# Rotating retention's keys and queries beside the input projection: halves swapped by DMA, products on GpSimd

## The reference, cut to what matters

```
q = _rotary(rq, pos)                       # (x1, x2) -> (x1 cos - x2 sin, x1 sin + x2 cos)
k = _rotary(rk, pos) * HEAD_DIM ** -0.5    # x1, x2: first and second half of each head's 64
for each chunk of 128 tokens, per head:
    att = (q @ k.T) * dmat
    o = att @ v + (q @ s) * q_dec
    s = s * c_dec + (k * k_dec).T @ v
```

## Time and profile before

| | us |
|---|---|
| median of 3 runs | 1070.62 |
| lowest, highest | 1069.22, 1072.57 |
| the profiled execution's own time | 1070.89 |
| its span, first to last instruction | 1069.1 |
| PE busy in the span | 974.4 (91%) |
| DVE busy | 628.9 (59%) |
| ACT busy | 344.7 (32%) |
| POOL busy | 109.6 (10%) |
| mean granted PE clock, as a share of full speed | 0.956 |
| data moved, mean rate | 267.07 MB, 250 GB/s |

### The profile page before, as it was taken

The page is one execution under the profiler, slowest core; times in us unless marked ns, Lnnn a source line. Parts: engine busy times, 40 slices in busy tenths (PEclk is TensorE's granted clock), DMA queues, the critical chain, the costliest instruction groups (busy, mean ns, idle before and its releaser), DMA issues.

```text
span 1069.1 us, 20936 instructions
## 1 busy us (share of the span) xinstructions
PE 974.4 (91%) x7883; PEld 680.2 (64%) x7883; DVE 628.9 (59%) x1077; ACT 344.7 (32%) x742; POOL 109.6 (10%) x105
## 2 busy tenths in 40 slices
PE   2879999999999868788985999999999999999996
PEld 1557775666766545455653767677777777777775
DVE  1576875676676488685677486433465555554244
ACT  3512132334334325433234233242224222221113
POOL 0011111000001143213311121000000000000000
PEclk9899999999999889879996899999999999999998
DMA  9978877877777888777996668877666998787662
GB/s 319 343 252 284 284 248 277 281 244 265 257 261 226 276 297 331 276 262 242 348 340 201 221 207 266 248 230 233 202 197 161 233 236 236 223 240 247 202 211 83
DMA packets 216434, 267.07 MB, mean 250 GB/s; under 512 B 12961, under 2 KB 167913, under 8 KB 208146
## 3 DMA queue, kind: packets, MB, share of 16 engines
q1 hardware_dynamic: 108706, 124.26, 36.4%
q10 hardware_dynamic: 98416, 74.40, 22.7%
q0 software_dynamic: 9216, 67.11, 17.2%
HBM read 260.11 MB, written 5.64 MB: 249 GB/s over the span
## 4 chain that ended last, share of the span: by engine, by line
PE 74%; DVE 12%; ACT 4%; issue 2%; DVEq 2%; DMA 2%; SPq 1%; POOL 1%; ACTq 0%
PE banks L1085 14%; PE banks L1086 12%; PE banks L1087 12%; PE banks L1035 6%; PE banks L1173 5%; PE banks L1118 4%; PE banks L1098 4%; DVE KT L1795 4%; PE banks L1100 3%; PE banks L1099 3%; PE banks L1299 2%; DVEq L1687 2%; DMA xs<-in_x_sample 1%; PE banks L1291 1%; PE banks L1284 1%
## 5 line engine op out<-in xcount | busy, mean ns | idle before, releaser
L621 ACT ACTIVATE whi<-raw 128x1024 fp32r<-128x1024 f32 (+1 forms) x76 | 78.6, 1035 | 300.3 <-PE banks L1087 163.0
L1085 PE MATMUL banks<-ahi,whi 128*128 128x512 f32 x416 | 169.3, 407 | 2.9 <-DVE alo L1751 2.9
L1795 DVE STREAM_TRANSPOSE KT<-K 128x2048 f32<-128x2048 f32 x64 | 147.8, 2309 | 29.5 <-DMA K<-in_cache_k,kidx 14.8
L1087 PE MATMUL banks<-ahi,rawlo 128*128 128x512 f32 x416 | 163.2, 392 | 0.0
L1086 PE MATMUL banks<-alo,whi 128*128 128x512 f32 x416 | 163.2, 392 | 0.0
L1758 DVE TENSOR_TENSOR rawlo<-raw,whi 128x1024 fp32r<-128x1024 f32 (+1 forms) x76 | 91.7, 1207 | 52.4 <-ACT whi L621 49.7
L505 POOL DMA_INDIRECT K<-in_cache_k,kidx x64 | 65.7, 1026 | 509.5 <-DVE KT L1795 467.1
L1118 PE MATMUL banks<-KT,qbd 128*32 128x128 f32 x2048 | 77.0, 296 | 28.2 <-DVE KT L1795 26.9
L1085 PEld LDWEIGHTS banks<-ahi,whi 128*128 128x128 f32 x416 | 78.8, 189 | 33.7 <-issue 13.1
L1098 PE MATMUL banks<-ahi,whi 128*128 128x512 f32 x216 | 89.9, 416 | 1.2 <-DVE rawlo L1765 0.9
L1087 PEld LDWEIGHTS banks<-ahi,rawlo 128*128 128x128 f32 x416 | 78.7, 189 | 17.3
(11 more groups left out here) (318 smaller groups left out, 1454.7 us busy)
## 6 DMA issues: line engine op xcount, KB each, us to landing
V<-in_cache_v SPq DMA_DIRECT2D x184, 256.0 KB, 3.7
rawm<-in_w_mod ACTq DMA_DIRECT2D x14, 1024.0 KB
zT<-in_cache_v SPq DMA_DIRECT2D x52, 256.0 KB, 5.7
raw<-in_w_in ACTq DMA_DIRECT2D x12, 1024.0 KB, 7.1
raw<-in_w_gate ACTq DMA_DIRECT2D x22, 512.0 KB, 4.4
raw<-in_w_up ACTq DMA_DIRECT2D x22, 512.0 KB, 5.8
srw<-in_w_gate SPq DMA_DIRECT2D x22, 512.0 KB, 5.1
srw<-in_w_up SPq DMA_DIRECT2D x22, 512.0 KB, 6.6
```

Source lines behind the costliest of these rows:

```text
L621: act.activation(whi[t % 2][:, 0:kd, :], raw[u][:, 0:kd, t % 2 * P:(t % 2 + 1) * P], ACT.Copy).then_inc(s_hi, 1)
L1085: pe.matmul(out[:, :], whi[t % 2][:, k, :], hi(k), start=(first and n == 0), stop=False)
L1087: last = pe.matmul(out[:, :], low[:, k, :], hi(k), start=False, stop=(final and n == kd - 1))
L1795: dve.transpose(KTb[:, :, :, :], Kb[g % 2][:, :]).then_inc(s_kt, 1)
```

## The change

- The rotation moves from retention's slots to the projection's. Right after ACT has copied a tile of retention's k or q to `zT`, ACT issues four DMAs of 32 partitions (64 KB each) that write the tile with its halves exchanged to `swapped` (`swap_halves`; two buffers). GpSimd then does all three operations: `swapped` times `sin` (with the sign now in the constant), `zT` times `cos`, and their sum into `zT` (`rotate(m)`), behind the gather of key group m + 4. The rotation matmuls, DVE's two products and two sums per pair, and `scr`'s first two planes are gone; the readers take `zT`.
- `cos` and `sin` (512 KB) are loaded by SP near the start, into the last two tiles of retention's v region; `swapped` lies in the first two. So `keep_z` of those tiles waits for the last rotations.
- Value group 27 gets buffers of its own (ring 5: two planes of `scr`, two of the place that `cos` and `sin` left) and waits only for the last modulation chunk; group 29 is then the first in the `zT` tiles of k, after the last scores (`s_ra`).
- In retention's slots: ACT stages MoBA's heads ahead of the k copy; DVE does `decayed` ahead of `act_lo`; the PE's wait for the decayed scores moves to the third slot; in the last pair DVE does `stage_heads`, then the turn of the keys, then `select`, then `act_lo` and `split_out`.
- In the first `w_out` tile `turn_heads(3)` stands before the fifth group of three matmuls and not before the last.

```diff
-RING_2 = {g: 1 if g < 26 else 2 if g < 32 else 3 if g < 53 else 4 for g in range(17, NG, 2)}
+RING_2 = {g: 1 if g < 26 else 5 if g == 27 else 2 if g < 32 else 3 if g < 53 else 4 for g in range(17, NG, 2)}
...
-    put("sin", np.sin(ang))
+    put("sin", np.sin(ang) * np.where(p % 64 < 32, -1.0, 1.0)[:, None])
...
+    swapped, ctr = at(ZT + RV * T, "swapped", [P, 2, T]), at(ZT + (RV + 2) * T, "ctr", [P, 2 * T])
+    free = at(RAWM + 1024, "free", [P, 2, T])
...
+        sp.wait_ge(s_md, NMA)
+        sp.dma_start(ctr[:, :], const[:, NB:NB + 2 * T]).then_inc(s_const, 16)
...
             if g == 27:
-                sp.wait_ge(s_rk, 2 * HP)
+                sp.wait_ge(s_md, NMOD)
+            if g == 29:
+                sp.wait_ge(s_ra, HP)
...
-        def cosines(hp):
...
+        def rotate(m):
+            z, other = zT[:, Z_OF[m], :], swapped[:, m % 2, :]
+            pool.wait_ge(s_swap[m % 2], 64 * ((m - M_TURN) // 2 + 1))
+            pool.tensor_tensor(other, other, C("sin"), ALU.mult)
+            pool.tensor_tensor(z, z, C("cos"), ALU.mult)
+            pool.drain()
+            pool.tensor_tensor(z, z, other, ALU.add)
+            pool.drain().then_inc(s_rk, 1)
...
-            if g > R_PAIR and (g - R_PAIR - 1) % 3 == 0 and g <= R_PAIR + 10:
-                cosines((g - R_PAIR - 1) // 3)
+            if M_TURN <= g - 4 < M_TURN + 2 * HP:
+                if g - 4 == M_TURN:
+                    pool.wait_ge(s_const, 32)
+                rotate(g - 4)
...
         def keep_z(m):
             act.wait_ge(s_ft, m + 3)
+            if Z_OF[m] in (RV, RV + 1):
+                act.wait_ge(s_rk, 2 * HP - 1 + Z_OF[m] - RV)
             act.activation(zT[:, Z_OF[m], :], DB[:, :], ACT.Copy).then_inc(s_ev, 1)
+
+        def swap_halves(m):
+            n = m - M_TURN
+            act.wait_ge(s_ev, m + 3)
+            if n >= 2:
+                act.wait_ge(s_rk, n - 1)
+            for q in range(4):
+                src, dst = slice(32 * q, 32 * q + 32), slice(32 * (q ^ 1), 32 * (q ^ 1) + 32)
+                act.dma_start(swapped[dst, m % 2, :], zT[src, Z_OF[m], :]).then_inc(s_swap[m % 2], 16)
...
                 keep_z(s - 1)
+            if M_TURN < s <= M_TURN + 2 * HP:
+                swap_halves(s - 1)
             if n > 0:
                 probs_t(n - 1)
...
+            if hp >= 2:
+                for k in (2 * hp, 2 * hp + 1):
+                    stage_block_heads(k, KT + k - 4)
             if hp:
                 keep_heads(hp - 1)
...
-                if last_in is not None and n == kd - 1:
+                if last_in is not None and n == kd // 2:
...
-        def rotate(hp):
-            for n, sec in enumerate((RK, RQ)):
-                pe.matmul(bank[n][:, :], C("rot"), zT[:, sec + hp, :], start=True, stop=True).then_inc(s_rr, 1)
...
-            pe.wait_ge(s_rad, hp + 1)
-            if hp < HP - 1:
-                rotate(hp + 1)
-            else:
+            if hp == HP - 1:
+                pe.wait_ge(s_rad, hp + 1)
                 turn_heads(0)
                 turn_heads(1)
...
-        def rotated(hp):
-            if hp:
-                dve.wait_ge(s_rq, hp)
-            for n in range(2):
-                dve.wait_ge(s_rr, 2 * hp + n + 1)
-                tt(stage[n][:, :], bank[n][:, :], C("sin"), ALU.mult)
-            dve.drain()
-            for n, sec in enumerate((RK, RQ)):
-                dve.wait_ge(s_rc, 2 * hp + n + 1)
-                tt(scr[:, 1 - n, :], stage[n][:, :], zT[:, sec + hp, :], ALU.add).then_inc(s_rk, 1)
```

More of the change, by code:

```diff
@@ L115, in constants @@
     put("causal", np.where(i[None, :] <= i[:, None], 0.0, -BIG))
-    rot = np.zeros((P, P))
-    for m in range(P):
-        if m % 64 < 32:
-            rot[m + 32, m] = -1.0
-        else:
-            rot[m - 32, m] = 1.0
-    put("rot", rot)
     inv = (f(10000.0) ** (-np.arange(32, dtype=f) / f(32))).astype(f)
@@ L841, in _ @@
             if hp >= 2:
[L842 to L846 removed]
+                for k in (2 * hp, 2 * hp + 1):
+                    stage_hi(k, KT + k - 4)
             slot(s + 1)
```

64 lines of the change are left out of this document (26 added, 38 removed).

## The result

The changed kernel takes 1078.13 us (median of 11 runs, 1068.27 to 1083.78), the kernel before 1070.62 beside it (11 runs, 1065.1 to 1073.68). The ratio is 1.0077, 95% interval 1.0052 to 1.0102. The forecast was 1063.5 with a range of 1051 to 1073. The profiled execution took 1078.13 us, its span is 1076.3, its mean clock 0.957.

A forecast was written before the change was run, and what follows sets the result against it. Retention was taken as bound by hand-overs between engines, the projection by the PE itself. The sum -18 + 6.8 + 3.5 + 0.5 = -7.2 us against 1070.89 gave 1063.7, predicted as 1063.5, range 1051 to 1073.

The forecast's parts named there:

- Issues on ACT's queue: Projection, slots 13 to 20: four DMA issues delay the probabilities' copy 1.6 us a slot; 6.8 us in sum, bounds 3 to 10.
- GpSimd's hold on DVE: Projection: GpSimd's rotation products delay DVE's small operations and so the exponentials; 3.5 us taken, bounds 0 and 17.5.
- rival 3: Projection, slots 14 to 20: negmax's scalar operation waits for both GpSimd products, 2.5 us each time, 17.5 in all; 1077.7; chance 0.13.
- The cap: Retention: 30.72 MB at 347 GB/s needs 88.5 us, so at most 19.5 of 108 us can go.
- the 18 us: Retention's total saving as forecast, taken close under the 19.5 us limit; its terms summed to 25.9; bounds 9.3 and 25.9.
- 5.9 us for the PE's products: Retention: the rotation matmuls of three pairs leave the PE's path, 1.98 us a pair, saving 5.9 us.
- 4.4 for the staging: Retention: ACT stages heads ahead of the k copy, so two PE waits of 2.2 us go, saving 4.4 us.
- 3.4 for the value pages: Retention: SP's 7.4 us wait to load value group 27 goes, and with it the PE's 3.4 us.
- What DVE gives back, 6.2 us: Retention: DVE's rotation goes, saving 4.2 us in slot 32 and 2 of the 7.6 us of key waits.
- The clock in retention, 6 us: Retention: with fewer stalls, half of some 12 us lost to the lowered PE clock comes back, 6 us.
- Transfers +0.5 and the constants 0: Projection: 2.1 MB more delays some value page, 0.5 us (0 to 3); loading constants at the start costs 0 (-1 to +1).
- Rival 1: Projection hides it all: ACT's sequencer works ahead, the PE feels 2 us of issues, DVE none; 1055; chance 0.17.

The follow-up runs named there:

- late swap: The changed kernel with ACT's four swap DMAs moved behind its copy of the turned probabilities, nothing else; 1057.44 us, ratio 0.9906 to the kernel before.

## Why the prediction was wrong, by its own steps

- **Issues on ACT's queue, "1.6 us in each slot"**: this step failed. Its mechanism was right, the size was not. Forecast 6.8 us with a bound of 10, measured 15.9 - 0.8 = 15.1 us of waits, and 12.8 - 0.8 = 12.0 with GpSimd's products left out. I took the cost of an issue from one that stood alone on the queue (0.41 us) and called 0.60 the longest, where 0.60 was what an issue right behind another takes. These take 0.51 to 1.71 us each, four of them 2.45 to 3.55, and the bytes don't matter. The slack that the sum took off by slots (0 in slot 19, 0.6 in slot 15) was not there either.
- **The clock, missing in the sum**: the text wrote "full clock kept" for the projection, and priced the clock in retention only, where it fell after a stall. The same reading applied to my own new waits would have added it. It cost 11.2 us, and is the larger part of the miss of 15.7.
- **GpSimd's hold on DVE**: 3.5 us forecast, rival 3 at 17.5. While ACT was late, leaving the products out gave 5.6 us of the whole time and 10.4 of the stretch; with ACT in order, 0 to 4. The rival's mechanism showed (4.04 us for copies of 1.29), but scalar operations over 2.5 us in most slots, its own mark, did not come: the longest is 2.12 us (with the late swap 2.64). The two costs are not to be added up: they delay the same probabilities. GpSimd's own time, 3.9 us a slot "with the drain", was also short: its operations take that, and the stand ahead of the sum another 2.1 to 5.2 us.
- **"Slack under the transfers"**: of retention's part the total was near and the terms were not. The cap was worked out for 108 us (30.72 MB), while the yardstick stretch of 104.1 us moves 29.46 MB; at 347 GB/s that is 84.9 us and not 88.5. Measured were 87.0, and 82.8 to 88.4 with that code, at up to 357 GB/s, above the rate of the cap. So the 18 us were near for a reason that the sum did not hold, and in part by luck. 5.9 us for the PE's products, 4.4 for the staging and 3.4 for the value pages each cost the stretch nothing when put back alone, about 6 together, and 10 with DVE's chain of all four pairs. Each row of waits had been read as time to be had; it was to be had once. That the transfers are what the slack lies under is argued from their rate (337 to 357 GB/s here, 304 with all put back); no run changed the transfers.
- **What DVE gives back, 6.2 us**: put back in pairs 1 to 3, nothing. Its 4.2 was also read off wrongly: 3.4 + 0.6 is 4.0, and the idle time ahead of the sums in the earlier trace rows, 0.9 us, is that of all four pairs together and not of each, 0.6 of it a wait for GpSimd's product.
- **The clock in retention, 6 us**: about 3 us came.
- **Transfers +0.5 and the constants 0**: nothing in the runs speaks against them; with the late swap stretch 14 is 3.5 us (median 5.4) over the kernel before, of which the rest of the products may be all.
- **Rival 1** (the projection hides it, 1055) describes the late swap: 1057.44. The order of two lines separates it from the kernel that was made, so its price for the issues, 2 us, was not right for this kernel (15.1).
- **The chances**: slower had 0.14, nearly all of it for rival 3, and none for a larger price of the issues with its clock. Rival 3 gave 1077.7, near the 1078.13 measured, but with 17.5 us for a mechanism that was worth 5.6 to 10.4; that nearness is luck.

## What to carry to other kernels

Where a DMA issue stands on an engine whose next operation feeds the critical path, count the issues, not the bytes, by a row of an issue that follows another (0.60 us and not 0.37 here), and put them behind that operation. A new wait on the PE costs itself and then, in these runs, from a third as much to as much again in slower matmuls, so a sum that adds waits needs the clock as a term. And where several rows of waits lie in a stretch whose transfers run near the best rate seen, do not add them up, and test the pieces together: alone, each of them was worth nothing, and all of them 10 us.

## What the runs showed of the hardware

- A swap of 32 partitions within SBUF takes ACT's queue 0.51 us for its quickest and 0.61 us for its median issue, up to 1.71 (2.42 with the late swap); with one issue a tile the median is 0.53. Other issues on the same queue that stood alone took 0.37 to 0.41 us in these slots, and 0.60 to 0.63 right behind another (`w_up`, 22 of them). What makes some of them up to three or four times as long was not found.
- GpSimd stands 2.1 to 5.2 us between its second product and the sum, where its drain is, 25.1 us in eight slots. The products themselves take 1.3 us each. Whether the drain or something else holds it was not tried. The longest:

```profile
172.84 1.30 POOL L534 TENSOR_TENSOR zT<-zT,ctr 128x512 f32<-128x512 f32 x1
179.33 1.26 POOL L536 TENSOR_TENSOR zT<-zT,swapped 128x512 f32<-128x512 f32 x1 [5.19 <-issue]
```

- DVE's scalar operation at 256.79 us, one instruction of 0.17 us when alone, took 2.12 us. It started inside GpSimd's first product (256.34 to 257.65 us) and ended at 258.91 with the second one (257.59 to 258.87). The Trainium skill (SBUF — State Buffer, Who interferes with whom) says that the engine that issues first holds the shared ports "for the whole instruction"; by that the wait would have ended with the first product, after 0.9 us. The trace does not agree with that bound, as it did not in the earlier trace rows.
